# A two-block transformer kernel: the mixer's differential heads start among the inverse transform's tiles, and its output takes two tiles side by side

## The chip, the cores and the metric

One core of a Trainium2 chip runs the whole program in one launch. The metric is the device time in microseconds, the median of several executions. The engines are TensorE (PE, with its weight loads as PEld), VectorE (DVE), ScalarE (ACT), GpSimd (POOL) and SyncE (SP), whose queue starts the transfers of weights.

## The reference

The reference is two blocks of two layers each over 512 latent tokens of width 1024 and 256 context tokens. The part that matters here is the first layer of the second block. Its mixer makes, from one modulated activation, the queries, keys and values of four differential heads and three streams of a long convolution ("hyena"), and joins both through one output matrix:

```python
s = einsum("bqhcd,bkhcd->bhcqk", q, k) * (ATT_QK_DIM ** -0.5)   # 4 heads, 2 score maps each, 768 keys
p = softmax(s, axis=-1)
w = p[:, :, 0] - lam * p[:, :, 1]
o = einsum("bhqk,bkhd->bqhd", w, v)
att = rmsnorm(o, subln_g) * (1.0 - lam_init)
hy = x0 * long_conv(v * x1, filt, bias)        # rfft, product, irfft, plus bias times input
y = concatenate([att, hy]) @ mix_w_out + mix_b_out
h = h + gate * y
```

After it come the MLP of the layer, a pooling layer, and a last normalisation.

## The kernel before

All large products are done in a split float form: each operand is held as a high part and a low part, and a product is three matrix products (high by high, high by low, low by high). Weights come as tiles of 128 x 1024. One tile is copied by SP's queue to one of four raw buffers; ScalarE copies it to one of three high buffers (`whi`, L486), VectorE subtracts to get the low part (`wlo`, L496). A slot of `whi` is free once TensorE is done with the tile that held it, a raw buffer once it is done with the tile four places ahead.

`tile_order` (L306) writes the order of all weight tiles and of the small conditioning products ("mod", L455) out by hand; every engine walks the same list, each at its own pace (`pe_tiles`, `act_tiles`, `dve_tiles`), and does what stands in it up to a named mark. A tile with `hold` 1 makes the conversion stay one tile less ahead, which is needed where two tiles are used side by side. Conditioning products collect in bank b7; a "turn" transposes a finished part in b6.

PSUM is used as ps0, ps1 and ps2 of 1024 columns each (two banks), and b6 and b7 of 512 (one bank). Each has a list of users: who claims it waits for the reads of the user before. `begin_stage` makes ScalarE, VectorE and GpSimd wait for the newest work of every engine, where SBUF is used anew.

The stretch of the change is written by four functions, in this order.

`long_convolution` (L2455 on) takes the transformed input through four forward tiles ("dft", L2485), whose results VectorE multiplies by the filter's spectrum (L2533 to L2547) and splits (L2513 on ScalarE, L2551 on VectorE), then through four inverse tiles ("idft", L2500), which all accumulate into the same four banks: both of ps2, b6 and b7. At its end, for each of the four parts j, VectorE adds the bias times the input (L2561), multiplies by x0 (L2565), ScalarE rounds to the high part (L2518), VectorE subtracts to get the low part (L2568).

`diff_attend` (L1220) does sixteen units, four heads of four blocks of 128 queries. A unit u is: two score maps on TensorE into ps0 and ps1 (L1013), the negated row maxima on VectorE (L1327), the exponentials with their sums on ScalarE (L1288), the reciprocals on VectorE (L1340, L1342), the scaling of the first map on GpSimd (L1403), the combination of both on VectorE (L1350), six transpositions on TensorE into ps2 (L1030), their copies to SBUF by ScalarE and VectorE (L1278, L1334), and the product with the values into b6 (L1247), which ScalarE copies and squares (L1296, L1301). The loop is staggered: in step u stand the scores of unit u, the transpositions of u-1 and the values of u-2. After each four units GpSimd makes the inverse root and scales the head's rows (L1380 to L1396); TensorE transposes them (L1255), ScalarE and VectorE make the high and low part (L1307, L1355). Its buffers are made anew behind a `begin_stage`.

`mixer_output` (L2668) waits for everything of both, then does eight output tiles one after the other, 24 products of 512 columns each (L2682), the four heads' parts first. VectorE scales the residual tile by tile (L2701) and adds the gated result (L609); ScalarE squares it for the next normalisation (L677).

Of the kernel before, what the change touches and what calls it, by code (L numbers as in the profile page):

```python
# [8 lines left out]
F32 = mybir.dt.float32  # L9
# [4 lines left out]
P = 128  # L14
NT = 512
# [290 lines left out]
def tile_order():  # L306
# [45 lines left out]
def program(nc, din, out, known):  # L352
# [867 lines left out]
    def diff_attend(tag, qp, kx, Vd, Yh, Yl, operands_at):  # L1220
# [4 lines left out]
        with ExitStack() as s:  # L1225
            E0 = [sb(s, [P, T]) for _ in range(2)]
            Pb = [sb(s, [P, T]) for _ in range(3)]
            PT = [sb(s, [P, 2, 3, P]) for _ in range(2)]
            y = [sb(s, [P, 4, P]) for _ in range(2)]
            sq = sb(s, [P, P])  # L1230
            ss = [sb(s, [P, 4]) for _ in range(2)]
            inv, half = [sb(s, [P, 4]) for _ in range(2)], [sb(s, [P, 4]) for _ in range(2)]
            gain, power = sb(s, [P, 1]), sb(s, [P, 4])
            begin_stage()

            def pe_diff():
                def turn_of(u):
                    PEQ.wait_ge(*at("dve_prob", (tag, u)))
                    pe_turn(tag, u, 0, units[u][0], Pb[u % 3])

                def values(u):
                    g, h, c = units[u]
                    for r in range(2):
                        PEQ.wait_ge(*turn_read_at(tag, u, 0, r, u == n - 1))
                    PEQ.wait_ge(*b6.claim((tag, "values", u)))
                    for r, b, kb in g["blocks"]:
                        ins = pe.matmul(b6.ap[:, 0:P], PT[u % 2][:, r, b, :], Vd[:, kb, P * h:P * h + P], start=kb == 0,  # L1247
                                        stop=kb == 5)
                    ins.then_inc(*up("pe_values", (tag, u)))

                def head(h):
                    PEQ.wait_ge(*at("pool_y", (tag, h)))
                    PEQ.wait_ge(*b6.claim((tag, "head", h)))
                    for c in range(4):
                        ins = pe.transpose(b6.ap[:, P * c:P * c + P], y[h % 2][:, c, :], mat("ident"))  # L1255
                    ins.then_inc(*up("pe_head", (tag, h)))

                for token in operands_at:
                    PEQ.wait_ge(*token)
                PEQ.wait_ge(*ps[2].claim((tag, "turns")))  # L1260
# [12 lines left out]
            def act_diff():  # L1273
                def turned(u):
                    ACTQ.wait_ge(*at("pe_turn", (tag, u, 0, 0)))
                    if u >= 2:
                        ACTQ.wait_ge(*at("pe_values", (tag, u - 2)))
                    act.activation(PT[u % 2][:, 0, :, :], ta.ap[:, 0:384].rearrange("p (b q) -> p b q", q=P),  # L1278
                                   ACT.Copy).then_inc(*turn_freed(tag, u, 0, 0, u == n - 1, "act"))

                def exponentials(u, j):
                    row, p = stat(u, j), (E0[u % 2], Pb[u % 3])[j]
                    ACTQ.wait_ge(*at("dve_max", (tag, u, j)))
                    if j == 0 and u >= 2:
                        ACTQ.wait_ge(*at("dve_prob", (tag, u - 2)))
                    if j and u >= 3:
                        ACTQ.wait_ge(*at("pe_turn", (tag, u - 3, 0, 1)))
                    act.activation(keys_of(p, FULL), scores_of(ps[j], FULL), ACT.Exp, bias=row[:, 7:8],  # L1288
                                   accum_out=row[:, 3:4]).then_inc(*ps[j].freed((tag, u), "act"))

                def values(u):
                    g, h, c = units[u]
                    ACTQ.wait_ge(*at("pe_values", (tag, u)))
                    if h >= 2:
                        ACTQ.wait_ge(*at("pe_head", (tag, h - 2)))
                    act.activation(y[h % 2][:, c, :], b6.ap[:, 0:P], ACT.Copy).then_inc(*up("act_y", (tag, u)))  # L1296
                    if u:
                        ACTQ.wait_ge(*b6.after((tag, "values", u - 1)))
                    if h >= 2 and c == 0:
                        ACTQ.wait_ge(*at("pool_root", (tag, h - 2)))  # L1300
                    act.activation(sq[:, :], b6.ap[:, 0:P], ACT.Square,  # L1301
                                   accum_out=ss[h % 2][:, c:c + 1]).then_inc(*b6.freed((tag, "values", u), "act"))

                def head(h):
                    ACTQ.wait_ge(*at("pe_head", (tag, h)))
                    ACTQ.wait_ge(*at("dve_gain", 0))
                    act.activation(Yh[:, h, :], b6.ap, ACT.Copy, scale=gain[:, :]).then_inc(*up("act_yhi", (tag, h)))  # L1307

                for u in range(n + 4):
                    if 1 <= u <= n:  # L1310
                        turned(u - 1)
                    if u < n:
                        exponentials(u, 0)
                        exponentials(u, 1)
                    if 2 <= u < n + 2:
# [6 lines left out]
            def dve_diff():  # L1322
                def maximum(u, j):
                    DVEQ.wait_ge(*at("pe_score", (tag, u, j)))
                    if u >= 3:
                        DVEQ.wait_ge(*at("dve_prob", (tag, u - 3)))
                    dve.tensor_reduce(stat(u, j)[:, 7:8], scores_of(ps[j], FULL), AX.XY, ALU.max,  # L1327
                                      negate=True).then_inc(*up("dve_max", (tag, u, j)))

                def turned(u):  # L1330
                    DVEQ.wait_ge(*at("pe_turn", (tag, u, 0, 1)))
                    if u >= 2:
                        DVEQ.wait_ge(*at("pe_values", (tag, u - 2)))
                    dve.tensor_copy(PT[u % 2][:, 1, :, :], tb.ap[:, 0:384].rearrange(  # L1334
                        "p (b q) -> p b q", q=P)).then_inc(*turn_freed(tag, u, 0, 1, u == n - 1, "dve"))

                def weights(u):
                    r0, r1 = (stat(u, j)[:, 7:8] for j in range(2))
                    DVEQ.wait_ge(*ps[0].after((tag, u)))
                    dve.reciprocal(r0, stat(u, 0)[:, 3:4]).then_inc(*up("dve_inverse", (tag, u)))  # L1340
                    DVEQ.wait_ge(*ps[1].after((tag, u)))
                    dve.reciprocal(r1, stat(u, 1)[:, 3:4]).then_inc(*up("dve_own"))  # L1342
                    DVEQ.wait_ge(*now("dve_own"))
                    dve.tensor_tensor(r1, r1, small[:, 34:35], ALU.mult).then_inc(*up("dve_own"))
                    DVEQ.wait_ge(*now("dve_own"))

                def combined(u):
                    p = Pb[u % 3][:, :]
                    DVEQ.wait_ge(*at("pool_e0", (tag, u)))
                    dve.scalar_tensor_tensor(p, p, stat(u, 1)[:, 7:8], E0[u % 2][:, :], ALU.mult,  # L1350
                                             ALU.add).then_inc(*up("dve_prob", (tag, u)))

                def head(h):
                    DVEQ.wait_ge(*at("act_yhi", (tag, h)))
                    dve.scalar_tensor_tensor(Yl[:, h, :], b6.ap, gain[:, :], Yh[:, h, :].bitcast(F32), ALU.mult,  # L1355
                                             ALU.subtract).then_inc(*b6.freed((tag, "head", h), "dve"))
# [3 lines left out]
                for u in range(n + 4):  # L1360
                    if u < n:
                        maximum(u, 0)
                        maximum(u, 1)
# [1795 lines left out]
```

## Time and profile before

| | us |
|---|---|
| median of 3 runs | 3222.01 (3219.78 to 3222.47) |
| the profiled execution | 3220.32 |
| its span | 3219.0 |
| TensorE busy | 3019.1 (94%) |
| VectorE busy | 1418.2 (44%) |
| ScalarE busy | 1072.9 (33%) |
| GpSimd busy | 313.1 (10%) |

Times in rows are microseconds from the start of the span, unless ns is written. A busy TensorE is not one at its peak: the granted clock (PEclk) is given beside it, 1.00 being 2.4 GHz and 0.50 being 1.2 GHz. The changed stretch lies between 2212 and 2357 us.

### The profile page before, as it was taken

Reading aid. Unit: us, or ns where it says so; the run is one execution under the profiler, and the core shown is the slowest. Engines: PE = TensorE matmul, PEld = TensorE weight load, DVE = VectorE, ACT = ScalarE, POOL = GpSimd, SP = SyncE. Lnnn points to the kernel's source line nnn. Section 1 sums busy time; section 2 is a strip of 40 time slices with the busy share of each in tenths; the row PEclk is TensorE's granted clock in tenths of the full one; section 3 lists DMA queues with packets and bytes.
Section 4 is the critical chain, followed back from the end, with each engine's and each line's share of the span. In section 5 each row is a group of like instructions: output and inputs, shape, how many; then the busy total and the mean of one; then the engine's idle time right before and its main releaser. Section 6 shows DMA issues by size and latency. Waiting matters only on the chain.

```text
span 3219.0 us, 41567 instructions
## 1 busy us (share of the span) xinstructions
PE 3019.1 (94%) x17128; PEld 2308.4 (72%) x17128; DVE 1418.2 (44%) x2184; ACT 1072.9 (33%) x1807; POOL 313.1 (10%) x334
## 2 busy tenths in 40 slices
PE   5989999999999988999999998997889999899998
PEld 3766657788888866766667776775567888678886
DVE  2556542423233345654444445536734444344443
ACT  3235441412122242553422335212533323342222
POOL 1012220300000030221201002000310000110000
PEclk7999999999999999999999999998989999889999
DMA  6313134222212122103343322422322232222322
GB/s 236 94 58 105 34 119 150 86 99 85 66 60 65 58 77 69 60 14 127 134 150 98 103 87 79 165 94 92 99 85 92 94 96 92 67 66 92 98 92 79
DMA packets 83876, 299.08 MB, mean 93 GB/s; under 512 B 9479, under 2 KB 11783, under 8 KB 83432
## 3 DMA queue, kind: packets, MB, share of 16 engines
q1 hardware_dynamic: 79200, 286.30, 27.2%
q10 hardware_dynamic: 4488, 10.12, 0.9%
q8 instruction: 137, 2.24, 0.3%
q14 instruction: 51, 0.42, 0.0%
HBM read 294.29 MB, written 2.10 MB: 92 GB/s over the span
## 4 chain that ended last, share of the span: by engine, by line
PE 87%; DVE 5%; ACT 4%; issue 2%; DMA 1%; POOL 1%; ACTq 0%; DVEq 0%; POOLq 0%
PE bank L592 42%; PE bank L596 21%; PE bank L1013 4%; PE bank L455 3%; PE bank L1030 3%; PE bank L1074 2%; PE bank L2682 2%; PE bank L1828 1%; PE bank L1566 1%; DMA t<-in_mod 1%; PE bank L1450 1%; PE bank L1022 1%; ACT t L1288 1%; ACT t L843 1%; ACT t L1112 1%
## 5 line engine op out<-in xcount | busy, mean ns | idle before, releaser
L592 PE MATMUL bank<-t 128*128 128x512 f32 (+1 forms) x6432 | 1757.3, 374 | 26.5 <-DVE t L2326 11.1
L592 PEld LDWEIGHTS bank<-t 128*128 128x128 f32 x6432 | 1113.0, 189 | 297.1 <-issue 69.1
L596 PE MATMUL bank<-t 128*128 128x512 f32 (+1 forms) x3216 | 1070.7, 372 | 5.9 <-POOL t L852 5.7
L596 PEld LDWEIGHTS bank<-t 128*128 128x128 f32 x3216 | 556.8, 189 | 127.4 <-POOL t L852 12.0
L486 ACT ACTIVATE t<-t 128x1024 fp32r<-128x1024 f32 x350 | 366.3, 1050 | 558.4 <-PE bank L596 497.5
L496 DVE TENSOR_TENSOR t<-t 128x1024 fp32r<-128x1024 f32 x350 | 430.5, 1234 | 262.4 <-ACT t L486 258.8
L609 DVE SCALAR_TENSOR_TENSOR t<-bank,t 128x512 f32<-128x512 f32 x192 | 129.8, 693 | 511.0 <-PE bank L596 484.2
L933 DVE TENSOR_TENSOR t<-t 128x512 f32<-128x512 f32 (+1 forms) x128 | 98.4, 769 | 335.8 <-ACT t L913 335.8
L913 ACT ACTIVATE t<-bank 128x512 f32<-128x512 f32 (+1 forms) x128 | 83.3, 651 | 418.7 <-PE bank L596 418.7
L1214 POOL TENSOR_SCALAR t<-t 128x768 f32<-128x768 f32 (+3 forms) x160 | 125.7, 788 | 576.3 <-DVE t L1182 576.3
L455 PE MATMUL bank<-t 128*32 128x256 f32 x1536 | 128.9, 414 | 33.7 <-DMA t<-in_mod 23.5
L1013 PE MATMUL bank<-t 64*128 64x384 f32 (+2 forms) x768 | 139.7, 483 | 20.8 <-ACT t L1288 9.9
L1030 PEld LDWEIGHTS bank<-t 128*128 128x128 f32 x880 | 97.2, 142 | 69.8 <-issue 37.4
L1030 PE MATMUL bank<-t 128*128 128x128 f32 x880 | 136.0, 284 | 11.5 <-DVE t L1168 6.3
L1157 DVE TENSOR_REDUCE t<-bank 128x1 f32<-128x768 f32 (+1 forms) x120 | 96.5, 845 | 106.2 <-PE bank L1022 76.5
L936 DVE TENSOR_TENSOR t<-t 128x512 fp32r<-128x512 f32 (+1 forms) x128 | 98.5, 769 | 96.2 <-ACT t L915 96.2
L1102 ACT ACTIVATE t<-bank 128x384 f32<-128x384 f32 (+1 forms) x160 | 73.5, 460 | 195.0 <-PE bank L1030 194.6
L677 ACT ACTIVATE t<-t 128x512 f32<-128x512 f32 (+1 forms) x64 | 43.8, 685 | 275.9 <-DVE t L609 192.6
L1112 ACT ACTIVATE t<-bank,t 128x768 f32<-128x768 f32 (+3 forms) x160 | 124.1, 780 | 9.3 <-DVE t L1154 3.9
L915 ACT ACTIVATE t<-t 128x512 fp32r<-128x512 f32 (+1 forms) x128 | 87.8, 686 | 108.1 <-DVE t L933 108.1
L1013 PEld LDWEIGHTS bank<-t 64*128 64x128 f32 x768 | 67.7, 193 | 65.7 <-issue 32.7
L852 POOL TENSOR_TENSOR t<-t 128x768 fp32r<-128x768 f32 (+1 forms) x24 | 39.9, 1662 | 734.4 <-ACT t L843 733.6
(289 smaller groups left out, 2281.4 us busy)
## 6 DMA issues: line engine op xcount, KB each, us to landing
t<-in_mod SPq DMA_DIRECT2D x192, 512.0 KB, 4.3
t<-in_l0fc SPq DMA_DIRECT2D x64, 512.0 KB, 3.5
t<-in_l1fc SPq DMA_DIRECT2D x64, 512.0 KB, 3.5
t<-in_s0fc SPq DMA_DIRECT2D x64, 512.0 KB, 3.5
t<-in_s1fc SPq DMA_DIRECT2D x64, 512.0 KB, 3.5
t<-in_mixin SPq DMA_DIRECT2D x24, 512.0 KB, 3.5
t<-in_l0in SPq DMA_DIRECT2D x12, 512.0 KB, 3.6
t<-in_l1in SPq DMA_DIRECT2D x12, 512.0 KB, 3.5
```

The source lines that it names most:

```text
L455: ins = pe.matmul(b7.ap[32 * j:32 * j + 32, 0:256], cond[:, k, :], modw[:, i % NM, 256 * j:256 * j + 256], start=k == 0, stop=k == NK - 1)
L486: act.activation(whi[:, a % NS, :], raw[:, a % NR, :], ACT.Copy).then_inc(*up("act_whi", a))
L496: dve.tensor_tensor(wlo[:, a % NR, :], raw[:, a % NR, :], whi[:, a % NS, :].bitcast(F32), ALU.subtract).then_inc(*up("dve_wlo", a))
L592: pe.matmul(acc.ap[:, o:o + m], w[:, ws], Hh[:, k, o:o + m], start=k == 0 and w is hi, stop=False)
L596: ins = pe.matmul(acc.ap[:, o:o + m], hi[:, ws], Hl[:, k, o:o + m], start=False, stop=k == NK - 1)
L609: ins = dve.scalar_tensor_tensor(x[:, o:o + n], acc.ap[:, o:o + n], mcol(L, part, k, s), x[:, o:o + n], ALU.mult, ALU.add)
L933: dve.tensor_tensor(r2[m % 2][:, 0:n], a, a, ALU.mult).then_inc(*up("dve_asq", (name, e)))
L936: dve.tensor_tensor(Al[:, m, :], r2[m % 2][:, 0:n], Ah[:, m, :].bitcast(F32), ALU.subtract).then_inc(*up("dve_alo", (name, q, m)))
L1013: ins = pe.matmul(ps[side].ap[:, 512 * r + o:512 * r + o + m], g["q"][side](c), g["k"][side][:, k0:k0 + m], start=r not in begun, stop=last)
L1030: ins = pe.transpose(turns[r].ap[:, P * b:P * b + P], p[:, P * i:P * i + P], mat("ident"))
L1112: act.activation(keys_of(p, g), scores_of(ps[side], g), ACT.Exp, bias=row[:, 7:8], accum_out=row[:, 3:4]).then_inc(*ps[side].freed((tag, u ...
L1214: pool.tensor_scalar(x, x, stat(u, side)[:, 7:8], 1.0, ALU.mult, ALU.mult).then_inc(*up("pool_prob", (tag, u, side)))
```

## The change

In `tile_order` the second output tile gets `hold` 1. `diff_attend` no longer writes its four engine programs itself; it returns for TensorE, ScalarE and VectorE the parts `early` (scores; exponentials; maxima, reciprocals and combination of a unit), `rest` (all else) and `head` (the last head's transposition and parts), and `long_convolution` calls them. TensorE does the scores of unit 0 after the first inverse tile and those of unit 1 after the third; ScalarE and VectorE do their parts of these units after the conversions that stand at the second and fourth inverse tile. At the end VectorE reads the four banks in a row; the products, the high parts and the low parts stand inside the units. The buffers E0 and Pb lie where the filter's spectrum (Kc, Ks) was, PT and y where the transformed values (Fh, Fl) were, and the second `begin_stage` is gone. In `mixer_output` tiles 0 and 1 run side by side, the hyena parts first and the last head at the end; the residual is scaled for all eight tiles ahead.

```diff
-        t.tile(("mixout", m))
+        t.tile(("mixout", m), m == 1)
...
+            def rest():                                  # TensorE
                 PEQ.wait_ge(*ps[2].claim((tag, "turns")))
-                for u in range(n + 4):
-                    if u < n:
+                for u in range(1, n + 2):
+                    if 2 <= u < n:
                         pe_scores(tag, u, units[u][0], units[u][2])
-                    if 1 <= u <= n:
+                    if u <= n:
                         turn_of(u - 1)
-                    if 2 <= u < n + 2:
+                    if u >= 2:
                         values(u - 2)
                     if u >= 7 and u % 4 == 3:
                         head((u - 7) // 4)
                     if u < n:
                         pe_tiles((tag, u))
...
+            def rest(high):                              # ScalarE
+                for u in range(1, n + 2):
+                    if u <= n:
+                        turned(u - 1)
+                    if 2 <= u < n:
+                        early(u)
                     if u >= 2:
+                        values(u - 2)
+                    if 2 <= u < 6:
+                        high(u - 2)
...
+            def early(u):                                # VectorE
+                if u == 0:
+                    dve.tensor_scalar(gain[:, :], v("subln"), ...)
+                maximum(u, 0)
+                maximum(u, 1)
+                weights(u)
+                combined(u)
+
+            def rest(product, low):
+                for u in range(1, n + 2):
+                    if 2 <= u < n:
+                        maximum(u, 0)
+                        maximum(u, 1)
+                    if u <= n:
+                        turned(u - 1)
+                    if 1 <= u < 5:
+                        product(u - 1)
+                    if 2 <= u < n:
+                        weights(u)
+                        combined(u)
+                    if 2 <= u < 6:
+                        low(u - 2)
...
+            for n_, q in enumerate((0, 2, 1, 3)):        # TensorE, inverse tiles
...
                     ins.then_inc(*up("pe_tile", i))
+                if n_ in (0, 2):
+                    pe_heads.early(n_ // 2)
+            pe_heads.rest()
...
+            for n_, q in enumerate((0, 2, 1, 3)):        # ScalarE, and so VectorE
+                act_tiles(("idft", q))
+                if n_ in (1, 3):
+                    act_heads.early(n_ // 2)
...
+            for j in range(4):                           # VectorE
+                bank = (ps[2], ps[2], b6, b7)[j]
+                dve.scalar_tensor_tensor(tmp[j][:, :], u[:, j, :], v("hbias", j), banks[j], ALU.mult,
+                                         ALU.add).then_inc(*bank.freed(("hy", "y"), "dve"))
...
+            keys = [("mixout", m) for m in range(NK)]    # TensorE, output
+            for these in (keys[0:2], *([key] for key in keys[2:])):
...
+                for k in (4, 5, 6, 7, 0, 1, 2, 3):
+                    if len(these) == 2:
+                        if k == 3:
+                            pe_head()
...
+                        PEQ.wait_ge(*hi_at)
+                        PEQ.wait_ge(*lo_at)
...
+            act_tiles(("mixout", 1))                     # ScalarE, after the Sqrt table
+            act_head()
...
+            dve_tiles(("mixout", 1))                     # VectorE
             for m in range(NK):
                 x = XT[m][:, 0:NT]
                 dve.tensor_scalar(x, x, small[:, 24 + m:25 + m], 1.0, ALU.add, ALU.mult).then_inc(*up("dve_own"))
-                DVEQ.wait_ge(*now("dve_own"))
+            dve_head()
+            DVEQ.wait_ge(*now("dve_own"))
+            for m in range(NK):
                 dve_tiles(("mixout", m))
```

## Rows read from the trace of the kernel before

**Rows 1.** The page, part 4: the chain that ended last, by engine.

```profile
PE 87%; DVE 5%; ACT 4%; issue 2%; DMA 1%; POOL 1%; ACTq 0%; DVEq 0%; POOLq 0%
```

**Rows 2.** Stretches: length, busy (count) by engine PE, PEld, DVE, ACT, POOL, clock.

```profile
2278.80:2325.00 46.20, 39.03 (x308) 26.20 (x306) 33.98 (x66) 25.89 (x74) 18.57 (x39) 1.00 0.33 100
...
2339.70:2345.00 5.30, 3.47 (x10) 2.62 (x11) 2.18 (x4) 3.12 (x4) 0.00 (x0) 0.50 0.00 0
```

**Rows 3.** Timeline, transforms: start, us, engine, line, operation, count [idle before <-releaser].

```profile
2177.10 0.66 PE L2472 MATMUL bank<-t 128*128 128x128 f32 x4 [1.38 <-DVE t L2631]
...
2181.05 1.97 PE L2472 MATMUL bank<-t 128*128 128x128 f32 x8 [2.10 <-DVE t L2523]
...
2212.17 11.19 PE L2500 MATMUL bank<-t 128*128 128x512 f32 x48
...
2219.14 0.68 DVE L2536 TENSOR_TENSOR t<-bank,t 128x512 f32<-128x512 f32 x1
...
2221.79 2.94 ACT L486 ACTIVATE t<-t 128x1024 fp32r<-128x1024 f32 x3
...
2224.26 11.24 PE L2500 MATMUL bank<-t 128*128 128x512 f32 x48 [0.91 <-ACT t L486]
```

**Rows 4.** Timeline from the last inverse tile to the first exponentials.

```profile
2235.54 0.75 DVE L2561 SCALAR_TENSOR_TENSOR t<-t,bank 128x512 f32<-128x512 f32 x1 [3.05 <-PE bank L2500]
2236.32 0.69 DVE L2565 TENSOR_TENSOR t<-t 128x512 f32<-128x512 f32 x1
...
2238.32 0.74 DVE L2561 SCALAR_TENSOR_TENSOR t<-t,bank 128x512 f32<-128x512 f32 x1
...
2239.16 2.93 PE L1013 MATMUL bank<-t 64*128 64x384 f32 x8 [3.66 <-issue]
...
2246.02 0.69 DVE L2568 TENSOR_TENSOR t<-t 128x512 fp32r<-128x512 f32 x1 [0.69 <-ACT t L2518]
...
2248.28 1.28 ACT L1288 ACT_TABLE_LOAD   x1 [2.29 <-DVE t L1327]
```

**Rows 5.** Timeline of a conditioning product and of one unit of differential attention.

```profile
2256.00 0.64 PE L455 MATMUL bank<-t 128*32 128x256 f32 x8
...
2259.35 1.82 DVE L1327 TENSOR_REDUCE t<-bank 128x1 f32<-128x768 f32 x2
...
2261.09 0.55 DVE L1334 COPY t<-bank 128x384 f32<-128x384 f32 x1
...
2261.80 0.90 POOL L1403 TENSOR_SCALAR t<-t 128x768 f32<-128x768 f32 x1 [3.84 <-DVE t L1340]
...
2262.36 1.56 PE L1013 MATMUL bank<-t 64*128 64x384 f32 x8 [0.30 <-ACT t L1288]
...
2262.82 1.02 DVE L1350 SCALAR_TENSOR_TENSOR t<-t 128x768 f32<-128x768 f32 x1
...
2263.92 1.82 DVE L1327 TENSOR_REDUCE t<-bank 128x1 f32<-128x768 f32 x2
```

**Rows 6.** Timeline, GpSimd's power and the scaling behind it; the last power, alone.

```profile
2276.78 1.65 POOL L1382 TENSOR_TENSOR t<-t 128x4 f32<-128x4 f32 x1
...
2281.22 0.91 POOL L1403 TENSOR_SCALAR t<-t 128x768 f32<-128x768 f32 x1
...
2335.82 1.02 POOL L1382 TENSOR_TENSOR t<-t 128x4 f32<-128x4 f32 x1
```

**Rows 7.** Timeline from the last values to the second output tile.

```profile
2333.31 1.58 PE L1247 MATMUL bank<-t 128*128 128x128 f32 x12 [0.71 <-ACT t L1301]
...
2340.85 0.69 ACT L1307 ACTIVATE t<-bank,t 128x512 fp32r<-128x512 f32 x1 [5.39 <-PE bank L1255]
...
2341.57 0.75 DVE L1355 SCALAR_TENSOR_TENSOR t<-bank,t 128x512 fp32r<-128x512 f32 x1 [10.17 <-ACT t L1307]
...
2342.64 8.15 PE L2682 MATMUL bank<-t 128*128 128x512 f32 x24 [1.83 <-issue]
...
2351.29 5.86 PE L2682 MATMUL bank<-t 128*128 128x512 f32 x24
```

More of the change, by code:

```diff
@@ L1224, in diff_attend @@
         n = len(units)
[L1225 to L1256, printed above, removed]
@@ new lines, in diff_attend, with pe_diff, turn_of, values @@
+        @dataclass
+        class Steps:
+            early: object
+            rest: object
+            head: object
+        def pe_diff():
+            def turn_of(u):
+                PEQ.wait_ge(*at("dve_prob", (tag, u)))
+                pe_turn(tag, u, 0, units[u][0], Pb[u % 3])
+            def values(u):
+                g, h, c = units[u]
+                for r in range(2):
+                    PEQ.wait_ge(*turn_read_at(tag, u, 0, r, u == n - 1))
+                PEQ.wait_ge(*b6.claim((tag, "values", u)))
+                for r, b, kb in g["blocks"]:
+                    ins = pe.matmul(b6.ap[:, 0:P], PT[u % 2][:, r, b, :], Vd[:, kb, P * h:P * h + P], start=kb == 0,
+                                    stop=kb == 5)
+                ins.then_inc(*up("pe_values", (tag, u)))
+            def head(h):
+                PEQ.wait_ge(*at("pool_y", (tag, h)))
+                PEQ.wait_ge(*b6.claim((tag, "head", h)))
+                for c in range(4):
+                    ins = pe.transpose(b6.ap[:, P * c:P * c + P], y[h % 2][:, c, :], mat("ident"))
+                ins.then_inc(*up("pe_head", (tag, h)))
+            def early(u):
@@ L1271, in pe_diff @@
                         pe_tiles((tag, u))
-            def act_diff():
-                def turned(u):
-                    ACTQ.wait_ge(*at("pe_turn", (tag, u, 0, 0)))
-                    if u >= 2:
[L1277 to L1315, printed above, removed]
@@ L1320, in act_diff @@
                         act_tiles((tag, u))
[L1322 to L1342, printed above, removed]
-                    DVEQ.wait_ge(*now("dve_own"))
[L1344 to L1356, printed above, removed]
-                dve.tensor_scalar(gain[:, :], v("subln"), (1.0 - LAM_INIT) * P ** 0.5, 1.0, ALU.mult, ALU.mult).then_inc(*up("dve_gain", 0))
@@ L1408, in diff_attend, with pool_diff, root @@
-            pe_diff()
-            act_diff()
-            dve_diff()
-            pool_diff()
+            return Steps(early, rest, lambda: head(3))
+        def pool_diff():
+            def root(h):
+                x, r, t = ss[h % 2][:, :], inv[h % 2][:, :], half[h % 2][:, :]
+                POOLQ.wait_ge(*b6.after((tag, "values", 4 * h + 3)))
+                pool.tensor_scalar(x, x, P * SUB_EPS, 1.0, ALU.add, ALU.mult).then_inc(*up("pool_own"))
+                POOLQ.wait_ge(*now("pool_own"))
+                pool.tensor_tensor(r, x, power[:, :], ALU.pow).then_inc(*up("pool_own"))
+                POOLQ.wait_ge(*now("pool_own"))
+                pool.tensor_scalar(x, x, -0.5, 1.0, ALU.mult, ALU.mult).then_inc(*up("pool_own"))
+                pool.tensor_tensor(t, r, r, ALU.mult).then_inc(*up("pool_own"))
+                POOLQ.wait_ge(*now("pool_own"))
+                pool.tensor_tensor(t, t, x, ALU.mult).then_inc(*up("pool_root", (tag, h)))
+                POOLQ.wait_ge(*at("pool_root", (tag, h)))
+                pool.tensor_scalar(t, t, 1.5, 1.0, ALU.add, ALU.mult).then_inc(*up("pool_own"))
+                POOLQ.wait_ge(*now("pool_own"))
+                pool.tensor_tensor(t, t, r, ALU.mult).then_inc(*up("pool_own"))
+                POOLQ.wait_ge(*now("pool_own"))
+                for c in range(4):
+                    row = y[h % 2][:, c, :]
+                    POOLQ.wait_ge(*at("act_y", (tag, 4 * h + c)))
+                    ins = pool.tensor_scalar(row, row, t[:, c:c + 1], 1.0, ALU.mult, ALU.mult)
+                ins.then_inc(*up("pool_y", (tag, h)))
+            pool.memset(power[:, :], -0.5).then_inc(*up("pool_own"))
+            for u in range(n):
+                x = E0[u % 2][:, :]
+                POOLQ.wait_ge(*at("dve_inverse", (tag, u)))
+                pool.tensor_scalar(x, x, stat(u, 0)[:, 7:8], 1.0, ALU.mult, ALU.mult).then_inc(*up("pool_e0", (tag, u)))
+                if u >= 5 and u % 4 == 1:
+                    root((u - 5) // 4)
+            root(3)
@@ L1415, in mixer_memory @@
+        steps = pe_diff(), act_diff(), dve_diff()
+        return (*steps, pool_diff), [x.head for x in steps]
     def mixer_memory(nq):
@@ L2657, in mixer_layer @@
         Yhh, Yhl = sb(S, [P, 4, NT], F32R), sb(S, [P, 4, NT], F32R)
-        long_convolution(x0, u, Kc, Ks, Yhh, Yhl)
+        tmp = [sb(S, [P, 512]) for _ in range(4)]
+        smalls = dict(sq=sb(S, [P, P]), ss=[sb(S, [P, 4]) for _ in range(2)], inv=[sb(S, [P, 4]) for _ in range(2)],
+                      half=[sb(S, [P, 4]) for _ in range(2)], gain=sb(S, [P, 1]), power=sb(S, [P, 4]))
+        with ExitStack() as here:
+            Fh, Fl = sb(here, [P, 8, 512], F32R), sb(here, [P, 8, 512], F32R)
```

369 lines of the change are left out of this document (205 added, 164 removed).

## The prediction

> **What bounds the kernel.** I read the chain of waits first: 87% of the span is TensorE's own work [rows 1], so an edit pays only where TensorE stands still or runs at half clock. The edits touch one stretch, the mixer from the inverse transform to its output, 2212 to 2357 us, so I read its timeline next, engine by engine. The reader should see three things in it.
>
> First, the seam after the inverse transform. Its last tiles end at 2235.50; then VectorE reads the four output banks one at a time, each followed by a product, ScalarE's high part and a low part, from 2235.54 to 2246.71 [rows 4]. TensorE gets its transposition bank (ps2) back only after the second read, at 2239.06, runs the first scores at half clock (2.93 us), and the first row maximum stands in VectorE's queue behind all of this. Second, the sixteen units of differential attention. Their period is a loop of latencies, 4.57 us from the maxima at 2259.35 to those at 2263.92: maxima, two exponentials, the next scores (1.56 us). VectorE is nearly full beside it: its combination ends at 2263.84, 0.08 us before the next maximum starts [rows 5]. Third, the seam to the mixer's output: the last values end at 2334.89, then GpSimd's root and scaling, the last head's transposition, its high and low part, and only at 2342.64 the first output tile, whose 24 products take 8.15 us at a clock that starts at 0.50, where the next take 5.86 [rows 2, 7].
>
> **Scores of units 0 and 1 among the inverse tiles.** A tile of 24 products takes 11.24/2 = 5.62 us [rows 3]. Tile one runs from 2212.17 to 2217.8. The scores of unit 0 claim ps1, which VectorE frees with its fourth product on the last forward tile, 2219.14 + 0.68 = 2219.82 [rows 3]: TensorE, which ran through here before, now waits 2.05 us. This wait is new; behind it stands the second inverse tile and nobody else. Then: scores 1.56 [rows 5], to 2221.45; two tiles to 2232.7; scores of unit 1, 2234.3; last tile to 2239.9. The 0.91 us which the third tile waited for its weights [rows 3] is covered (they are ready at about 2224.2, the tile starts at 2227.1). So the transform ends 2.05 + 2 x 1.56 - 0.91, about 4.4 us later, with the gaps rounded.
>
> Is anything late for it? ScalarE and VectorE convert tiles three and four first (ScalarE from 2221.79 [rows 3], VectorE to about 2225.3). Then VectorE has maxima 0 to 2227.1. ScalarE waits for the first, 2226.3, loads the table (1.28 us [rows 4]) and ends its exponentials at about 2229.7, before the scores of unit 1 want their banks at 2232.7. Maxima 1 run from 2235.2 (behind the low part of the second output tile, whose slot opens with inverse tile three), and by the unit's own offsets [rows 5] combination 1 ends 4.5 us on, 2239.7: just under the last inverse tile. The gain and GpSimd's power constant are of no weight, and its scalings find it idle. Keys and queries were placed long before. The table load and a second conversion lie under TensorE's tiles: nothing. If the cover were gone, the 1.28 us would stand on the path at the most.
>
> **The seam to the units.** VectorE now reads four banks in a row, 0.75 us each, starts some 0.7 apart, from 2239.94 [rows 4]: ps2 free at 2241.4, b7 at 2242.8. TensorE turns unit 0 at 2241.4, waits for b7 (the conditioning product needs it), then does two such products of 0.64 [rows 5] and the small transposition between them; I estimate 1.9 us for these three, to 2244.8. Scores of unit 2: to 2246.4, and maxima 2 start then, against 2259.35 before. Gain so far 12.95 us. This is the largest term, and it assumes full clock: 1.5 us of idle time, after a busy transform. Near rows: after 1.38 us idle four transpositions took 0.66, the full speed; after 2.10 us eight took 1.97, one part of them slow [rows 3]; after 3.66 us the scores took 2.93 [rows 4]. I take the first, the nearest, and keep the other end: 1.37 for the scores and by the same ratio 1.4 for turn and conditioning, 2.8 us; the wait of 2.05 us inside the transform could cost the same way up to 8.15 - 5.86 = 2.3 [rows 7]. No row shows a gain here.
>
> **The moved hyena products and low parts.** Four products and four low parts at 0.69 each [rows 4], starts 0.61 to 0.65 apart, leave the seam and go into units 1 to 5. The product stands before the reciprocals: the copy of the turned half ends 2.29 us after the maxima start, the product at 2.98, the first reciprocal and GpSimd's 0.90 us follow, and the combination starts at 4.25 instead of 3.47 [rows 5]. The low part comes behind it. So the next maximum comes at 5.97 instead of 4.57: 1.4 us for each of units 2, 3, 4. In unit 5 only a low part is left, 0.6; unit 1 lies in the seam. After unit 5 GpSimd's root and scaling for head 0 hold up the scaling of unit 6: it starts at 2281.22, where units without a root start theirs 2.45 us after their maxima [rows 5, 6]; the 0.6 us goes into that wait. Sum: 3 x 1.4 = 4.2 us lost. Bounds: 0, if VectorE found room for them; 4 x 1.43 = 5.7, if nothing is absorbed. ScalarE's four high parts, about as long, fit into its idle time (busy 25.89 of 46.20 us [rows 2]): nothing. From unit 6 on the order is the same, 12.95 - 4.2 = 8.75 us earlier.
>
> The power on GpSimd took 1.65 us beside VectorE's combination and 1.02 alone [rows 6]. The Trainium skill (SBUF — State Buffer, "Who interferes with whom") states that a VectorE instruction with two SBUF inputs blocks a GpSimd instruction that reads SBUF; the trace agrees. By that rule the low part behind combination 5, which has two such inputs, would hold the root of head 0 another 0.6 us, and the gain would be 15.6 instead of 16.2.
>
> **The mixer's output.** Tiles 0 and 1 run together: hyena parts, heads 0 to 2, 42 of 48 products, before the last head is wanted. From the last values' end, 2334.89 [rows 7]: a conditioning product 0.64 and gaps, 0.9; 42 x 0.2375 = 9.98, to 2345.8. The last head is scaled by 2339.65, long before. Then its transposition (0.63 at full clock, an estimate by [rows 3]'s 0.66), ScalarE 0.69, VectorE 0.75 [rows 7] with hand-overs of 0.1: TensorE waits for these, and 6 more products of 1.6 end at 2349.6. Before, the second tile ended at 2351.29 + 5.86 = 2357.15. Gain 7.5 us. What leaves is most of the 7.75 us between the last values and the first product, and the 2.3 us of half clock in it [rows 2, 7]. The table load for the root, the conversion of tile 2 and the eight scalings of the residual (VectorE, from about 2336) lie under the 42 products. The new order of VectorE puts its last head behind these scalings: free by some 2343, wanted at 2347. Tile 2's bank and weights are free; tile 3's high part waits for tile 0's slot and two squares, is ready by 2354 and wanted at 2356. The output tiles' DMAs go out in pairs instead of one by one, the conditioning ones behind them in SP's queue; each has over 5 us to land. Nothing. Bounds: 4 (a stall of 2 to 3 us at tiles 2 or 3) to 8.
>
> **Sum.** 8.75 + 7.5 = 16.2 us. The profiled execution took 3220.3 (span 3219.0 and 1.3 around it), giving 3204.1; the median of the runs is 1.7 above it, so I predict 3205.8.
>
> **Rivals.**
> (a) The clock falls at one of the new pauses (2.05 us inside the transform, 1.5 at the seam). For: the rows after 2.10 us. Against: those had thin work before them. Price 2.8 to 5.1: 3208.6 to 3210.9. Chance 0.18.
> (b) The early heads give nothing, the output alone pays: VectorE, already full in a unit, takes the moved work at double price in units 2 to 5, or the late transform does it. For: 0.08 us of room. Against: the moved work is 5 us in all. Time 3222.0 - 7.5 = 3214.5. Chance 0.11.
> (c) Slower: the stretched units (TensorE's busy share sinks from 39.03/46.20 = 84% [rows 2] to 0.84 x 4.57/5.97 = 65%) let the clock fall, and it stays low. At half clock a unit's work of 0.84 x 4.57 = 3.86 us takes twice that, 7.7 instead of 4.57 us, 3.1 a unit; it decides from the sixth such unit (16.2/3.1 = 5.2), and over all fourteen gives 3205.8 + 44 = 3250. Against: units from 2278.80 to 2325.00 ran at 1.00 with 39.03 of 46.20 us busy [rows 2]. For it speaks the Trainium skill (TensorE: Matmul & The Clock Gate, "Part 4: PE-mode transpose"), by which transpositions do not count as activity in the same way; each unit holds six among its scores, values and conditioning. The trace does not bear it out in this stretch. Chance 0.05.
> (d) It moves nothing that can be told, since a stall of another kind (a weight slot, a conditioning weight not landed) eats both: 3218. Chance 0.05.
>
> The forecast has 0.61; its own range is 3202 to 3209. The range for 8 in 10 takes in (a) and the bounds of the moved work below (16.2 + 4.2: 3201.6), and stops short of (b): 3200 to 3213.5. About 0.2% (6.4 us) is what a measurement can tell from no change: faster by more 0.89, within 0.06, slower 0.05.
>
> **What would show it.** Right: scores of unit 0 start near 2219.9; the transform ends near 2239.9; maxima 2 near 2246.4, and three periods near 6.0 before they return to 4.57; the first output product within 1.5 us of the last values; one wait of about 1.7 us before the last six products, and no slow products behind it. Wrong: scores of 2.93 us at the seam (a); periods above 6.5 (b); a granted clock of 0.5 in the units (c); waits at output tiles 2 or 3 (d).

## The result and the profile after

| | us |
|---|---|
| predicted | 3205.8 (3200.0 to 3213.5) |
| measured, changed kernel | 3203.22 (3200.48 to 3204.52, 4 runs) |
| kernel before, 4 runs | 3221.55 (3219.78 to 3222.47) |
| ratio | 0.9946, 95% interval 0.9934 to 0.9958 |
| profiled span | 3201.1 (before 3219.0) |

The change is faster by 0.54%. The spans differ by 17.9 us. Of these, 1.77 lie ahead of the first inverse product (2210.40 against 2212.17), where the programs do the same (a conditioning transfer issued at 150.33 us before is issued at 148.00, so a difference stands there almost from the start of the execution); 16.80 lie between it and the end of the second output tile (128.18 us against 144.98); behind it the changed kernel loses 0.67. So 16.8 us is what the edits moved in this pair of traces. The other 1.1 us of the span lie outside the stretch, and no run ties them to an edit; the medians differ by 18.3 us, so by them it is 1.5 us outside it, just as unexplained.

The shares in the chain of waits are hardly other than before, since TensorE's work is the same. Page, part 4, changed kernel:

```profile
PE 88%; DVE 5%; ACT 4%; issue 2%; DMA 1%; POOL 1%; ACTq 0%; DVEq 0%; SPq 0%; POOLq 0%
```

The timeline of the changed kernel from the inverse transform to unit 2 (start, us, engine, line, operation, count, idle time before and what ended it), which answers to [rows 3, 4]:

```profile
2210.40 5.67 PE L2521 MATMUL bank<-t 128*128 128x512 f32 x24
...
2217.38 0.68 DVE L2565 TENSOR_TENSOR t<-bank,t 128x512 f32<-128x512 f32 x1
...
2218.20 1.56 PE L1013 MATMUL bank<-t 64*128 64x384 f32 x8 [2.13 <-DVE t L2565]
...
2232.39 5.79 PE L2521 MATMUL bank<-t 128*128 128x512 f32 x24
...
2236.66 1.02 DVE L1361 SCALAR_TENSOR_TENSOR t<-t 128x768 f32<-128x768 f32 x1
2238.21 2.72 DVE L2592 SCALAR_TENSOR_TENSOR t<-t,bank 128x512 f32<-128x512 f32 x4 [0.53 <-PE bank L2521]
2239.67 0.87 PE L1030 MATMUL bank<-t 128*128 128x128 f32 x6 [1.50 <-DVE t L2592]
...
2240.99 0.64 PE L455 MATMUL bank<-t 128*32 128x256 f32 x8 [0.44 <-DVE t L2592]
...
2242.03 1.08 PE L455 MATMUL bank<-t 128*32 128x256 f32 x8
...
2243.04 2.60 PE L1013 MATMUL bank<-t 64*128 64x384 f32 x8
...
2245.68 1.82 DVE L1338 TENSOR_REDUCE t<-bank 128x1 f32<-128x768 f32 x2 [3.30 <-PE bank L1013]
```

The new wait of the first scores for ps1 is there, 2.13 us. The combination of unit 1 (L1361) ends at 2237.68, half a microsecond before the last inverse product at 2238.18. The four reads take 2.72 us together. The first conditioning product still takes 0.64 us, the second takes 1.08, and the scores of unit 2 take 2.60 instead of 1.56. That is half clock, at the seam after all, and VectorE stands still for 3.30 us in front of the maxima of unit 2.

A unit with a hyena product (L2599) and a low part (L2604) in it, same view, against [rows 5]; and GpSimd's power and the scaling behind it, against [rows 6]:

```profile
2247.88 0.68 DVE L2599 TENSOR_TENSOR t<-t 128x512 f32<-128x512 f32 x1
...
2248.73 0.90 POOL L1429 TENSOR_SCALAR t<-t 128x768 f32<-128x768 f32 x1 [12.18 <-DVE t L1351]
...
2249.74 1.02 DVE L1361 SCALAR_TENSOR_TENSOR t<-t 128x768 f32<-128x768 f32 x1 [0.81 <-POOL t L1429]
2250.68 0.68 DVE L2604 TENSOR_TENSOR t<-t 128x512 fp32r<-128x512 f32 x1
2251.28 1.81 DVE L1338 TENSOR_REDUCE t<-bank 128x1 f32<-128x768 f32 x2
...
2264.91 0.90 POOL L1429 TENSOR_SCALAR t<-t 128x768 f32<-128x768 f32 x1 [4.08 <-DVE t L1351]
...
2266.18 1.65 POOL L1408 TENSOR_TENSOR t<-t 128x4 f32<-128x4 f32 x1
...
2270.61 0.91 POOL L1429 TENSOR_SCALAR t<-t 128x768 f32<-128x768 f32 x1
```

The period, from the start of one unit's maxima to the start of the next unit's, is 2251.28 - 2245.68 = 5.60 us. The output, against [rows 7]:

```profile
2322.71 1.57 PE L1244 MATMUL bank<-t 128*128 128x128 f32 x12 [0.72 <-ACT t L1304]
...
2324.78 10.06 PE L2744 MATMUL bank<-t 128*128 128x512 f32 x42
...
2327.63 2.82 POOL L1422 TENSOR_SCALAR t<-t 128x128 f32<-128x128 f32 x4
2328.59 3.71 DVE L2768 TENSOR_SCALAR t<-t 128x512 f32<-128x512 f32 x8
2334.68 0.60 PE L1252 MATMUL bank<-t 128*128 128x128 f32 x4
...
2336.94 1.64 PE L2744 MATMUL bank<-t 128*128 128x512 f32 x6 [1.66 <-DVE t L1366]
```

There are 42 products under which GpSimd scales the last head, one wait of 1.66 us, and no slow products.

### The profile page after: what moved, and what is told of

Same layout as the page of the kernel before. It is cut to its first block, busy times and chain, and to the rows that moved or that the text cites. A ratio compares the mean times of both kernels' runs of the same rounds, so it can differ in the third digit from the quotient of the medians.

```text
span 3201.1 us, 41567 instructions
## 1 busy us (share of the span) xinstructions
PE 3015.2 (94%) x17128; PEld 2305.5 (72%) x17128; DVE 1416.9 (44%) x2184; ACT 1072.9 (34%) x1807; POOL 310.8 (10%) x334
## 4 chain that ended last, share of the span: by engine, by line
PE 88%; DVE 5%; ACT 4%; issue 2%; DMA 1%; POOL 1%; ACTq 0%; DVEq 0%; SPq 0%; POOLq 0%
PE bank L592 42%; PE bank L596 21%; PE bank L1013 4%; PE bank L455 3%; PE bank L1030 3%; PE bank L1074 3%; PE bank L2744 1%; PE bank L1852 1%; PE bank L1590 1%; DMA t<-in_mod 1%; PE bank L1474 1%; PE bank L1022 1%; ACT t L843 1%; ACT t L1112 1%; PE bank L653 1%
```

## The experiments

Below, the stretch is the time from the first inverse product to the end of the last output product: 185.9 us before, 169.1 in the changed kernel. Offsets (+) count from the first inverse product, "maxima 2" are the row maxima of unit 2, and the period of unit 2 is the time from maxima 2 to maxima 3. The expectations of the first four runs use a shorter stretch, to the end of the second output tile: 144.98 us before, 128.18 in the changed kernel. hyena_in_seam, one_tile, products_in_seam, hyena_on_pool, hyena_on_pool_2, scores_later, filled and output_barrier stand on one execution each, and every stretch is that of one execution, so it carries what the clock did in it.

**seam_only** undoes the output:

```diff
-            for these in (keys[0:2], *([key] for key in keys[2:])):
+            pe_head()
+            for token in (at("act_hyhi", 3), at("dve_hylo", 3), at("act_yhi", ("diff", 3)), b6.after(("diff", "head", 3))):
+                PEQ.wait_ge(*token)
+            for these in ([key] for key in keys):
...
-                for k in (4, 5, 6, 7, 0, 1, 2, 3):
...
+                for k in range(NK):
...
```

> The changed kernel with the mixer's output as before: the last head first, eight tiles one after the other, heads' parts first, the residual scaled tile by tile. Measured in the stretch from the first inverse product to the end of the second output tile (144.98 us before, 128.18 changed). Theory, the two parts add up: the last values end 8.8 us earlier than before, and the output keeps its wait of 7.7 us and its slow first products, so the stretch is 136.1 and the time about 3213. Rival, the output pays only since the seam was mended (or the other way round): the stretch is within 1.5 us of 128.2 or of 145.0.

3210.81 us, ratio 0.9974 (0.9964 to 0.9985); stretch 177.2, so 8.7 gained of 16.8; to the second output tile it is 136.25, where 136.1 was expected. The last values end at +113.97, in the changed kernel at +113.88, and the old gap is back:

```profile
2327.95 1.43 POOL L1422 TENSOR_SCALAR t<-t 128x128 f32<-128x128 f32 x4
2329.43 1.12 PE L1252 MATMUL bank<-t 128*128 128x128 f32 x4 [4.83 <-POOL t L1422]
...
2332.38 8.16 PE L2740 MATMUL bank<-t 128*128 128x512 f32 x24 [1.82 <-issue]
```

**output_only** undoes the seam: scores of units 0 and 1 in `rest`, the hyena tail in one piece.

```diff
-                if n_ in (0, 2):
-                    pe_heads.early(n_ // 2)
...
-                for u in range(1, n + 2):
-                    if 2 <= u < n:
+                for u in range(n + 2):
+                    if u < n:
                         pe_scores(tag, u, units[u][0], units[u][2])
...
```

> The changed kernel with the seam as before: scores of units 0 and 1 behind the transform, reads, products, high and low parts one after the other between them. Theory: the stretch is 144.98 - 7.96 = 137.0 us, the time about 3213.5; the first scores are slow (2.93 us) again. Rival: the moved order of the output gains nothing by itself, 143 or more.

3208.94 us, ratio 0.9970 (0.9960 to 0.9979); stretch 176.2, so 9.7 gained, and 135.3 to the second output tile, where 137.0 was expected. (The profiled execution took 3217.00; its first inverse product came at 2218.39, so what it is longer lies ahead of the stretch.) 8.0 us lie at the output as expected, 1.7 before the maxima of unit 1, which had not been expected: they came at +40.59, before at +42.35. The two parts add up to 8.7 + 9.7 = 18.4 against 16.8, so about 1.6 us are gained by either part alone and only once by both. **output_barrier** asks where it comes from:

```diff
+                if j == 0 and u == 0:
+                    ACTQ.wait_ge(*at("dve_hylo", 3))
                 ACTQ.wait_ge(*at("dve_max", (tag, u, j)))
```

> As output_only (the seam as before), with one wait more: ScalarE's first exponential waits for the last low part. output_only gained 9.7 us and not 8.0, the 1.7 before the maxima of unit 1 (40.58 instead of 42.3 after the transform's start): ScalarE loaded the exponential's table at 2252.23, before the first maximum was ready, where the kernel before waited at its stage's beginning and loaded it behind the maximum. Theory: with the wait the load stands behind the maximum again, maxima 1 at 42.3. Rival: the load is hoisted above any wait on one instruction, 40.6 as before, and the 1.7 us came from something else of the stage's beginning.

The edit is against output_only. Maxima 1 came at +41.93, and the stretch is 177.6. ScalarE in output_only, and then with the wait:

```profile
2252.23 1.28 ACT L1293 ACT_TABLE_LOAD   x1
...
2253.03 1.82 DVE L1340 TENSOR_REDUCE t<-bank 128x1 f32<-128x768 f32 x2
```

```profile
2245.43 1.82 DVE L1342 TENSOR_REDUCE t<-bank 128x1 f32<-128x768 f32 x2
2246.46 1.28 ACT L1295 ACT_TABLE_LOAD   x1 [1.86 <-DVE t L1342]
```

So 1.3 of the 1.7 us is the load of the exponential's table. In these two runs it stands ahead of the maximum where ScalarE has one wait in front of the exponential, and behind it where it has two. The last 0.4 us stays open.

**hyena_in_seam** leaves the products and low parts where they were:

```diff
+                dve.tensor_tensor(t, t, x0[:, j, :], ALU.mult).then_inc(*up("dve_hy", ("y", j)))
+                DVEQ.wait_ge(*at("act_hyhi", j))
+                dve.tensor_tensor(Yl[:, j, :], t, Yh[:, j, :].bitcast(F32), ...)
...
-            dve_heads.rest(product, low)
+            dve_heads.rest(lambda j: None, lambda j: None)
```

> The changed kernel, but products, high and low parts stay at the end of the transform, each behind its bank's read. It tells what moving them into the units is worth beside the early units. Theory: b7 comes free only 9.1 us after the transform's end, the two conditioning products and the scores of unit 2 follow at half clock, so maxima 2 start about 14.6 us after the transform instead of 7.5; in return units 2 to 5 have periods of 4.57 again (3.5 us). Stretch 128.2 + 7.1 - 3.5, about 131.8. Rival: moving them only shifts VectorE's load, which is the same 8 x 0.6 us either way: within 1 us of 128.2.

Stretch 173.0, 3.9 more than the changed kernel, and 132.1 in the terms of the expectation (131.8). Maxima 2 came at +42.20 instead of +35.28, with periods of 4.57 behind them. The conditioning product waits for VectorE's read of b7 until +36.92, in the changed kernel until +30.59:

```profile
2242.39 1.51 PE L1030 MATMUL bank<-t 128*128 128x128 f32 x6 [3.61 <-DVE t L2595]
...
2247.93 1.08 PE L455 MATMUL bank<-t 128*32 128x256 f32 x8 [4.03 <-DVE t L2595]
```

Moving the eight instructions is worth 3.9 us in this pair. VectorE does the same work in both; it pays because the banks come free sooner.

**one_tile** takes the pairing away and keeps the order:

```diff
-            for these in (keys[0:2], *([key] for key in keys[2:])):
+            for these in ([key] for key in keys):
...
```

> The changed kernel with the output tiles one by one, but hyena parts first and the last head last in tile 0. It tells what the pairing is worth apart from the order. 21 products of tile 0 cover 5.0 us; the last head's rows were scaled 4.8 us after the last values before, 6.2 in the changed kernel, where GpSimd's four scalings took 2.82 us beside VectorE's eight residual scalings and not 1.42. Theory: TensorE waits about 1.0 to 1.4 us longer, nothing else: stretch 129.2 to 129.6. Rival, the pairing does the work: the wait of 5 us that 21 further products covered comes back, 131 or more.

From the last values to the end of the second output tile it took 17.63 us; the changed kernel took 14.30, the kernel before 22.26. TensorE waited 1.32 us for GpSimd, within the forecast, then 1.96 for the head's parts, and then the clock fell, which neither side had:

```profile
2330.11 2.82 POOL L1422 TENSOR_SCALAR t<-t 128x128 f32<-128x128 f32 x4
...
2332.98 0.66 PE L1252 MATMUL bank<-t 128*128 128x128 f32 x4 [1.32 <-POOL t L1422]
...
2335.59 0.94 PE L2744 MATMUL bank<-t 128*128 128x512 f32 x3 [1.96 <-DVE t L1366]
2336.46 1.08 PE L455 MATMUL bank<-t 128*32 128x256 f32 x8
...
2337.47 6.93 PE L2744 MATMUL bank<-t 128*128 128x512 f32 x24
```

The stretch to this tile's end is 131.7 us, past the forecast of 129.2 to 129.6. The pairing gives 3.3 us of the output's 8.0 in this pair of executions and the order the other 4.6. But 1.5 of the 3.3 us are half clock (1.08 instead of 0.64 in the conditioning product, 6.93 instead of 5.86 in the tile), which one execution does not show to come every time; the other 1.8 are in the main the waits (1.32, and 1.96 instead of 1.66).

**products_in_seam** puts all four products into VectorE's idle time at the seam:

```diff
-                    if 1 <= u < 5:
-                        product(u - 1)
+                    if u == 1:
+                        for j in range(4):
+                            product(j)
```

> The changed kernel with all four hyena products behind the copy of turned unit 0, in the 3.30 us in which VectorE waits for the scores of unit 2; the low parts stay in the units. Theory, in a full unit every VectorE instruction is paid at its start-to-start time of 0.60 us: periods of units 2 to 4 fall from 5.60 to 5.00, maxima 2 stay, maxima 6 come 1.8 us earlier. Rival, the products are hidden in the period and the combination waits for GpSimd in any case (0.81 us of idle time before it): no change of the periods.

Periods of 5.01, 5.00, 4.98: 0.60 us a product, as the first theory said. Stretch 167.2.

**hyena_on_pool** and **hyena_on_pool_2** give both to GpSimd:

```diff
                 pool.tensor_scalar(x, x, stat(u, 0)[:, 7:8], ...).then_inc(*up("pool_e0", (tag, u)))
+                if u in (1, 2, 3, 4, 6):
+                    POOLQ.wait_ge(*at("dve_prob", (tag, u)))
+                if 1 <= u < 5:
+                    product(u - 1)
+                if 2 <= u < 5 or u == 6:
+                    low(min(u - 2, 3))
...
```

These lines are hyena_on_pool_2's. In hyena_on_pool the wait stands in units 1 to 5 and the low parts in units 2 to 5, so the last one is ahead of the root of head 0.

> The changed kernel with the hyena products and low parts on GpSimd, each behind the combination of its unit, so that they run beside the maxima, which read PSUM. Theory: periods of units 2 to 5 go back to 4.57, 3.5 us gained by maxima 6, if each of GpSimd's two instructions takes about 1.1 us (1.66 us for 768 columns elsewhere in this kernel) and both end before its next scaling is wanted, 2.9 us after the combination. Rival (the Trainium skill, SBUF - State Buffer, Who interferes with whom: a VectorE instruction that uses the shared port and a GpSimd one that reads SBUF block each other): GpSimd's chain is held up by VectorE's copies and the scaling of the next unit comes late; periods of 5.6 or more, and nothing is gained.

The periods of units 2 to 5 are 4.57, though GpSimd's scaling waited for the low part in front of it, but then 7.50 and 8.60: the root stood behind combination 5 and a low part of 1.28 us. Stretch 170.3, worse than the changed kernel. GpSimd in a unit:

```profile
2253.27 1.27 POOL L2601 TENSOR_TENSOR t<-t 128x512 f32<-128x512 f32 x1 [1.22 <-DVE t L1361]
...
2254.49 1.27 POOL L2606 TENSOR_TENSOR t<-t 128x512 fp32r<-128x512 f32 x1
...
2255.74 0.91 POOL L1425 TENSOR_SCALAR t<-t 128x768 f32<-128x768 f32 x1
```

> As hyena_on_pool, with the last low part behind combination 6 instead of 5, so that the root of head 0 stands directly behind the scaling of unit 5. There units 2 to 5 had periods of 4.57, but unit 6 came 7.5 and unit 7 8.6 us after the one before (5.10 and 6.26 in the changed kernel). Theory, the root waited for combination 5 and the low part: now 5.5 and 6.3, and maxima 8 come 3.1 to 3.5 us earlier than in the changed kernel. Rival, GpSimd is full with this work whatever its order, and the 4.6 us come back in units 6 to 8.

Behind four periods of 4.57 now stand 5.60 and 6.27; from maxima 2 to maxima 8 it took 30.16 us, 33.14 in the changed kernel. So 3.0 us are gained, a little less than the 3.1 to 3.5 expected. The stretch is 164.5; it met no half clock at either pause, which is the other 1.6 us.

**scores_later** and **filled** take one pause each:

```diff
-                if n_ in (0, 2):
-                    pe_heads.early(n_ // 2)
+                if n_ in (1, 2):
+                    pe_heads.early(n_ - 1)
```

> The changed kernel with the scores of unit 0 behind the second inverse tile instead of the first. Theory: the wait of 2.13 us for ps1 goes, as VectorE frees it while the second tile runs; unit 0's maxima start where they did (VectorE is busy with weights until then), and the transform ends 2.1 us sooner (25.65 instead of 27.78 after its start), as does everything behind it. Rival: VectorE's and ScalarE's chain for unit 1 then sets the reads of the four banks (combination 1 ended 0.5 us before the transform), and the gain is 1.0 or less.

The transform ended at +25.6, the wait was gone, maxima 2 came at +31.49. Stretch 165.4, that is 3.7 less: 2.2 of the wait, 1.5 because no clock fell in this execution.

```diff
+            PEQ.wait_ge(*ps[0].after(("diff", 1)))
+            pe.matmul(ps[0].ap[:, 0:512], mat("ones"), x0[:, 0, :], start=True, stop=True)
+            pe.matmul(ps[0].ap[:, 512:768], mat("ones"), x0[:, 1, 0:256], start=True, stop=True)
             pe_heads.rest()
```

> The changed kernel with two products more, whose result nobody reads, into the free bank ps0 in the pause of 1.5 us behind the transform (x0 by the matrix of ones, 512 and 256 columns, about 1.5 us by 1.02 us for two such of 512 in this kernel). Theory: the clock fell in this pause, so the conditioning product takes 0.64 instead of 1.08 and the scores of unit 2 1.56 instead of 2.60; maxima 2 come 1.6 us earlier (33.7 after the transform's start). Rival: the half clock is left over from the whole thin stretch and comes all the same: 35.3.

Maxima 2 came at +33.70, 1.58 sooner, the scores took 1.56 us, and the stretch is 167.6:

```profile
2239.74 1.02 PE L2528 MATMUL bank<-t 128*128 128x512 f32 x2
...
2242.72 0.64 PE L455 MATMUL bank<-t 128*32 128x256 f32 x8 [0.44 <-DVE t L2595]
...
2244.22 1.56 PE L1013 MATMUL bank<-t 64*128 64x384 f32 x8
```

One execution does not prove that filling did it, for hyena_on_pool_2 had no fall there either, without it. **changed_again** is the changed kernel beside the best version.

> The changed kernel once more, timed beside the version below on the same chip: about 3203. In the seven looks so far with the same pause of 2.1 us inside the transform the scores of unit 0 took 1.56 us in some and 2.93 in others, and where they took 2.93 the seam behind the transform ran at full speed. Theory, each execution loses about 1.6 us to half clock at one of the two pauses; rival, one of them may have none or both, and the stretch varies by 1.6 us.

3200.68 us, ratio 0.9937 (0.9925 to 0.9950). The first pause brought the fall this time, a little late, two tiles in 12.82 us instead of 11.28, and the seam ran at full speed:

```profile
2218.71 1.56 PE L1013 MATMUL bank<-t 64*128 64x384 f32 x8 [2.13 <-DVE t L2565]
2220.20 12.82 PE L2521 MATMUL bank<-t 128*128 128x512 f32 x48
...
2243.97 0.64 PE L455 MATMUL bank<-t 128*32 128x256 f32 x8
2244.54 1.56 PE L1013 MATMUL bank<-t 64*128 64x384 f32 x8
```

Of the nine profiled executions with that pause the clock fell there in four (one_tile, products_in_seam, hyena_on_pool, this), two at the seam (the changed kernel, seam_only), hyena_in_seam in its long pauses behind the transform, and two at neither pause (filled, hyena_on_pool_2). In none did it fall at both the first pause and the seam. scores_later, which has the seam's pause alone, kept the clock too. Other pauses are a case of their own: one_tile lost the clock again at its wait of 1.96 us in the output, and seam_only in its gap there. That each execution must lose it once is refuted by hyena_on_pool_2.

**both_and_filled** joins scores_later, hyena_on_pool_2 and filled.

> The changed kernel with the scores of unit 0 behind the second inverse tile, the two idle products at the seam, and the hyena products and low parts on GpSimd, the last low part behind the root of head 0. Theory, the single gains add up from the changed kernel's 169.1 us (first inverse product to the last product of the output): 2.1 for the pause, 1.6 for the clock, 3.5 for periods of 4.57 in units 2 to 5, so 161.9, and the time about 3196. Rival: with GpSimd's work in them the units are no shorter in total (its root comes late for unit 6), 165.5 as with the later scores alone.

3195.13 us, ratio 0.9922 (0.9909 to 0.9936); stretch 162.3 against 161.9 expected. It has the lowest median, 5.6 us under changed_again on the same chip. The intervals of the two ratios overlap. The stretches of the two traces differ by 6.8 us, of which 1.5 are the half clock that one of them met.

## Why the prediction was right, step by step

- **Transform.** 4.4 us later forecast, 4.45 measured (27.78 us against 23.33), and the wait for ps1 was the one named (2.13 us, 2.05 forecast). The early units' own work lay under TensorE's tiles, and the table load too; it stood ahead of the first maximum (2222.04, the maxima at 2223.51), not behind it as forecast.
- **Seam.** Maxima 2: 12.95 us earlier forecast, 11.9 measured (+35.28 against +47.18). The step that failed is the choice of full clock at the pause of 1.5 us. Half clock cost 1.04 in the scores, 0.44 in one conditioning product and some 0.1 in the small transposition, 1.6 in all, less than rival (a)'s 2.8: the turn of unit 0 and the first conditioning product were still fast. The 1.9 us for conditioning and transposition was 0.4 too long (1.5 at full clock in both_and_filled). So (a) was true in kind, its lower end too high, and its chance of 0.18 too low: of the seven executions that have both pauses the clock fell in six.
- **Moved hyena work.** Term mis-sized. Forecast 3 x 1.4, measured 1.03 (5.60 against 4.57). I had added whole durations; VectorE's instructions start 0.60 us apart at 0.68 each, the combination's successor 0.94 behind it at 1.02. The combination now waits for GpSimd as well (0.81 us of idle time before it). Unit 5 became 0.42 us longer (4.99), not 0.6, and unit 6 as much shorter (5.10 against 5.52 before), so this went into GpSimd's root as forecast. Net loss to maxima 7: 11.90 - 8.83 = 3.1 us instead of 4.2. The errors of this step and of the one before cancel (8.83 measured, 8.75 forecast), and that is luck: the forecast had the seam's gain 1.05 us too high and the units' loss 1.1 us too high.
- **The port.** The power took 1.65 us again with a low part right behind the combination, and the scaling of unit 6 started 5.70 us after that of unit 5, as before: the loss of 0.6 us that would have made 15.6 of the 16.2 did not come. In hyena_on_pool the power ran behind the combination and took 1.03. The 1.65 us beside the combination fits the Trainium skill's rule (SBUF — State Buffer, "Who interferes with whom"). Why the low part (2266.86 to 2267.54, inside the power's 2266.18 to 2267.83) did not hold the power longer stays open.
- **Output.** 7.5 forecast, 7.96 measured, the same wait (1.66). GpSimd's four scalings took 2.82 us, not 1.42, beside the residual's eight scalings (1.43 in seam_only without them). By the Trainium skill (SBUF — State Buffer, "Who interferes with whom") a VectorE `tensor_scalar` can hold the port that GpSimd needs; the traces agree (2.82 us beside eight of them, 1.43 without). With 42 products above it this was hidden; in one_tile, with 21, it was not.
- **Sum.** 16.2 forecast, 16.8 in the stretch. The median came 2.6 us under the forecast: 0.6 of it is this, 0.5 is that the kernel before was faster in its four runs than in the three used (3221.55, 3222.01), and 1.5 lie outside the stretch. Rival (b) fell (the seam alone gives 8.7 us), and so did (c): the granted clock from 2245.70 to 2264.00 was 1.00 with 14.90 of 18.30 us busy. That is 81%, not the 65% that (c) had worked out, so (c)'s own condition was never met. The 84% it started from were an average over units of 4.57 to 6.27 us; in three full units of the kernel before it was 94% (12.91 of 13.72 us, the third window below). The Trainium skill's rule on transpositions (TensorE: Matmul & The Clock Gate, "Part 4: PE-mode transpose") would speak for a fall; no run here shows one in these units. Windows (length, busy and count by engine, clock), two of the changed kernel, of which the second is the seam, and one of the kernel before:

```profile
2245.70:2264.00 18.30, 14.90 (x120) 10.73 (x120) 15.76 (x29) 10.95 (x29) 2.71 (x3) 1.00 0.32 107
```

```profile
2238.20:2245.70 7.50, 5.58 (x33) 2.51 (x34) 4.05 (x9) 0.49 (x1) 0.00 (x0) 0.77 0.57 162
```

```profile
2259.35:2273.07 13.72, 12.91 (x103) 8.85 (x103) 11.41 (x21) 8.25 (x24) 2.71 (x3) 1.00 0.36 93
```

## What to carry to other kernels

Where one phase ends in a row of reads, products and roundings, move only the reads to the front: what the next phase waits for is the bank, not the arithmetic (3.9 us here). In a nearly full loop price an instruction at its start-to-start time, and look for an engine with idle time in it (GpSimd here) before VectorE pays, but keep that engine's own long chain first in its queue. Put a new early step behind the point where its bank is free anyway: one tile later was 2.2 us better here.

## What was not expected of the hardware

The same pause of 2.1 us brought half clock in four of nine executions, and the changed kernel itself had it there in one profiled execution and not in the other. At either pause it cost 1.5 to 1.7 us, and in the four executions where it came at the first, the next pause of 1.5 us went without. What decides it no run here shows. A kernel with short pauses so has a spread of its own, as large as some of the edits here. And a table load may or may not be hidden behind a wait for reasons that are no part of the arithmetic: one wait more on ScalarE cost 1.3 us (output_barrier against output_only).
